# Layer 2's first modulation part summed under layer 1's mix, column chunks on VectorE, and a new order of transfers in a two-layer decoder trunk

## What is computed

```python
cond = jax.nn.silu(c)
for l in range(DEPTH):
    mod = (cond @ w_ada[l] + b_ada[l])[:, None, :]          # w_ada[l]: 1024 x 6144
    sh1, sc1, g1, sh2, sc2, g2 = jnp.split(mod, 6, axis=-1)
    h = x * (1.0 + sc1) + sh1
    u, q_lat, kv_lat, k_rope = jnp.split(h @ w_in[l], split_cols, axis=-1)
    # causal pooling of u, latent attention of q_lat, kv_lat, k_rope, 6 heads
    mixed = jnp.concatenate([pooled, attn], axis=-1) @ w_out[l]
    x = layer_norm(DEEPNORM_ALPHA * x + g1 * mixed, ln1_g[l], ln1_b[l])
    h = x * (1.0 + sc2) + sh2
    ffn = swiglu(h, shared weights) + routed_moe(h, ...)    # 64 experts, top 8
    x = layer_norm(DEEPNORM_ALPHA * x + g2 * ffn, ln2_g[l], ln2_b[l])
```

## Time and profile before

| | |
|---|---|
| median of 3 runs | 1358.78 us (1357.85 to 1361.09) |
| the profiled execution | 1359.6 us |
| its span in the trace | 1357.8 us |
| TensorE busy | 1281.2 us (94%) |
| VectorE busy | 462.8 us (34%) |
| ScalarE busy | 255.1 us (19%) |
| GpSimd busy | 160.9 us (12%) |
| moved by DMA | 495.83 MB, 365 GB/s over the span |

### The profile page before, as it was taken

The page is one execution under the profiler, slowest core; times in us unless marked ns, Lnnn a source line. Parts: engine busy times, 40 slices in busy tenths (PEclk is TensorE's granted clock), DMA queues, the critical chain, the costliest instruction groups (busy, mean ns, idle before and its releaser), DMA issues.

```text
span 1357.8 us, 28824 instructions
## 1 busy us (share of the span) xinstructions
PE 1281.2 (94%) x9667; PEld 796.8 (59%) x9667; DVE 462.8 (34%) x1096; ACT 255.1 (19%) x528; POOL 160.9 (12%) x589
## 2 busy tenths in 40 slices
PE   7989999899799999999898999999999999999995
PEld 3455566566466665666446557666666666656563
DVE  1264542222222222232427355222333222322235
ACT  1213211111111111111123312111111111111113
POOL 0000022111111111112000002012111111111110
PEclk8989999899899999999999999999999999999998
DMA  9998459999999999999989855769989999999992
GB/s 325 351 401 342 191 213 422 419 422 419 422 422 419 421 422 421 371 382 416 387 351 368 356 200 180 332 234 420 421 334 422 421 420 421 421 420 386 394 408 111
DMA packets 86679, 495.83 MB, mean 365 GB/s; under 512 B 14244, under 2 KB 22452, under 8 KB 31816
## 3 DMA queue, kind: packets, MB, share of 16 engines
q1 hardware_dynamic: 86600, 494.66, 90.1%
HBM read 493.55 MB, written 1.08 MB: 364 GB/s over the span
## 4 chain that ended last, share of the span: by engine, by line
PE 85%; DVE 5%; DMA 5%; issue 2%; SPq 1%; ACT 1%; POOL 0%; DVEq 0%; ACTq 0%; POOLq 0%
PE ps L999 31%; PE ps L1021 15%; PE ps L931 9%; PE ps L1042 8%; PE ps L941 4%; PE ps L647 4%; PE ps L864 4%; DMA ring<-in_w_ada 3%; DMA w<-in_w_ada 2%; PE ps L887 2%; DVE acc L1427 1%; PE ps L967 1%; PE ps L1014 1%; PE ps L947 1%; PE ps L830 1%
## 5 line engine op out<-in xcount | busy, mean ns | idle before, releaser
L999 PE MATMUL ps<-ring,w 128*64 128x256 f32 (+1 forms) x3776 | 426.4, 384 | 2.9 <-ACT w L1185 1.8
L999 PEld LDWEIGHTS ps<-ring,w 128*64 128x64 f32 (+1 forms) x3776 | 269.3, 127 | 73.4 <-issue 16.3
L1021 PE MATMUL ps<-ring,w 128*64 128x512 f32 (+1 forms) x944 | 215.0, 597 | 0.0
L999 PE MATMUL ps<-flex,w 128*32 128x256 f32 x736 | 169.2, 389 | 20.0 <-issue 19.7
L999 PE MATMUL ps<-w 128*32 128x256 f32 x736 | 169.7, 390 | 0.0
L1612 DVE SCALAR_TENSOR_TENSOR w<-ps,w 128x256 f32<-128x256 f32 x59 | 28.5, 484 | 384.8 <-PE ps L999 384.8
L931 PE MATMUL ps<-hx,scat 128*128 128x512 f32 x488 | 142.9, 417 | 0.9 <-issue 0.9
L1598 DVE CAST scat<-ps 128x512 fp32r<-128x512 f32 x118 | 81.7, 692 | 164.4 <-PE ps L1021 164.4
L1179 ACT ACTIVATE w<-ps 128x512 f32<-128x512 f32 x122 | 73.0, 598 | 298.8 <-PE ps L931 298.8
L999 PEld LDWEIGHTS ps<-flex,w 128*32 128x32 f32 x736 | 81.0, 112 | 77.5 <-issue 35.3
L1042 PE MATMUL ps<-scat 128*128 128x512 f32 x472 | 123.3, 403 | 0.0
(11 more groups left out here) (259 smaller groups left out, 1252.3 us busy)
## 6 DMA issues: line engine op xcount, KB each, us to landing
ring<-in_w_exp_gate SPq DMA_DIRECT2D x88, 1024.0 KB, 18.3
ring<-in_w_exp_up SPq DMA_DIRECT2D x88, 1024.0 KB, 20.7
ring<-in_w_exp_down SPq DMA_DIRECT2D x88, 1024.0 KB, 20.9
ring<-in_w_ada SPq DMA_DIRECT2D x30, 1024.0 KB, 10.1
flex<-in_w_exp_gate SPq DMA_DIRECT2D x20, 1024.0 KB, 12.4
w<-in_w_exp_gate SPq DMA_DIRECT2D x20, 1024.0 KB, 15.3
flex<-in_w_exp_up SPq DMA_DIRECT2D x20, 1024.0 KB, 14.0
w<-in_w_exp_up SPq DMA_DIRECT2D x20, 1024.0 KB, 17.1
```

Of the source, the lines that this page charges most:

```text
L999: last = mm(ps[unit * g:unit * g + unit, bank, 0:F], hTb[:, kt, unit * g:unit * g + unit], weights(k)[:, kt, :], start=kt == 0, stop=kt == ...
L1021: last = mm(ps[unit * g:unit * g + unit, bank, :], midT[:, f, unit * g:unit * g + unit], down_w(k)[:, f, half * 512:(half + 1) * 512], sta ...
```

## The change

Six things change.

1. In layer 1's start the chunk sums go to VectorE: eight operations of 128x512 per chunk (`scalar_tensor_tensor` into `acc0`), each linked to the one before. `turn_chunk` then adds all 128 partitions up by a product with ones.
2. Layer 2's part 0 is summed on VectorE in layer 1's mix (`next_part`): six of the eight tiles before `norm_stats` of token tile 0, two before that of tile 1. SP issues the tiles in two groups of four (`next_tiles`), one ahead of the stores of the modulation, one behind the column loads. 16 small matmuls behind the last piece of the mix make the columns, in place of the filler matmuls. All of this leaves the step between the layers.
3. The two column loads `g2_col` and `b2_col` move from layer 1's start to just ahead of the second group.
4. VectorE sums the first two tiles of part 1 (`gate_part((0, 1))`) ahead of its pooling and rotary work; `w_out` is loaded in two halves, one behind tile 5 and one behind tile 7 of part 1.
5. TensorE sums tiles 0 and 1 of part 2 between the scores of heads 1 and 2 and of heads 3 and 4, and tile 3 to 7 one in each of the first five heads.
6. The gathered tokens are transposed ahead of the second half of the shared expert's down product; `shmid` lies in `acc0` for that.

The core of the diff:

```diff
@@ SP, end of layer 1's attention and its mix
+                if l == 0:
+                    sp.wait_ge(s["acc0_zeroed"], 2)
+                    sp.dma_start(acc0[0:1, :], b_ada[1:2, 0:ADA_W]).then_inc(s["acc0_bias_in"], 16)
+                    next_tiles((0, 1, 2, 3))
                 store_mod(l, 1)
                 store_mod(l, 2)
                 mod_row(g_row, 2, s["rows1_in"])
...
+                if l == 0:
+                    for dst, src in ((g2_col, lay(ln2_g, 0)), (b2_col, lay(ln2_b, 0))):
+                        sp.dma_start(dst, src.rearrange("a (k p) -> p (a k)", p=P)).then_inc(s["cols2_in"], 16)
+                if l == 0:
+                    next_tiles((4, 5, 6, 7))
                 sp.wait_ge(s["pv_ready"], (l + 1) * H)
@@ SP, weights of a layer
-                ada_tiles(l, 1, (4, 5, 6, 7))
+                ada_tiles(l, 1, (4, 5))
+                load_w_out(0, 4)
+                ada_tiles(l, 1, (6, 7))
+                load_w_out(4, 8)
@@ VectorE, start of layer 1
-                        dve.wait_ge(s["p0_done"], c + 1)
                         part = acc0[:, c * CHUNK_W:(c + 1) * CHUNK_W]
-                        v.tensor_tensor(part, ps[:, 6, :], part, ALU.add).then_inc(s["p0_evicted"], 1)
+                        for kt in range(KT):
+                            if kt % 4 == 0:
+                                dve.wait_ge(p0_landed[2 * c + kt // 4], 32)
+                            ins = v.scalar_tensor_tensor(part, p0_chunk(c)[:, kt].rearrange("p h n -> p (h n)"), c32v[:, kt, 0:1], part,
+                                                         ALU.mult, ALU.add)
@@ VectorE, the mix
+                def next_part(kts):
+
+                    for kt in kts:
+                        n = NEXT_JOB + kt
+                        buf = n % ADA_BUFS
+                        dve.wait_ge(ada_landed[buf], (n // ADA_BUFS + 1) * 16)
+                        ins = v.scalar_tensor_tensor(acc0[:, :], ada_at[buf], c32v[:, kt, 0:1], acc0[:, :], ALU.mult, ALU.add)
+                        ins.then_inc(ada_used[buf], 1)
+                        dve.wait_ge(ada_used[buf], n // ADA_BUFS + 2)
...
                 mod_value(2, slice(0, 64)).then_inc(s["mod_val_ready"], 1)
+                if l == 0:
+                    dve.wait_ge(s["acc0_bias_in"], 48)
+                    next_part(range(6))
                 dve.wait_ge(s["cols_in"], (l + 1) * 64)
...
                 normalise(0, l * 2 * NT + 1).then_inc(s["t_ready"], 1)
+                if l == 0:
+                    next_part((6, 7))
+                    dve.sem_inc(s["p0_done"], 1)
@@ TensorE, behind the mix
-                keep_busy(0, 4)
+                if l == 0:
+                    pe.wait_ge(s["p0_done"], CHUNKS + 1)
+                    for i in range(2 * KT):
+                        last = mm(ps[:, 1, P0_COL + i:P0_COL + i + 1], acc0[:, i * P:(i + 1) * P], ones[:, 0:1], start=True, stop=True)
+                    last.then_inc(s["p0_columns"], 1)
+                else:
+                    keep_busy(0, 4)
@@ TensorE, between the layers
-                    for kt in range(KT):
-                        pe.wait_ge(p0_landed[kt], 48)
-                        for g in range(4):
-                            last = mm(ps[32 * g:32 * g + 32, 6, :], c32v[:, kt, :], next_p0[kt][:, g, :],
-                                      start=kt == 0, stop=kt == KT - 1)
-                    last.then_inc(s["p0_done"], 1)
                     turn_x2(0)
@@ TensorE, shared expert
                     if j == 0:
+                        pe.wait_ge(s["G_ready"], (b0 + l + 1) * 2)
+                        passed(pe)
+                        turn_gathered(b0, 0)
+                        turn_gathered(b0, 1)
                         pe.wait_ge(s["order_read"], l + 1)
```

More of the change, by code:

```diff
@@ L69 @@
 ADA_BUFS = 4
-ADA_JOBS = ((None, 0, 8), (None, 16, 24))
+ADA_JOBS = ((None, 0, 8), (None, 24, 32))
+NEXT_JOB = 16
 CHUNKS = 4
@@ L223, in decoder_trunk @@
         ada = [a.rearrange("p (g n) -> p g n", g=4) for a in ada_at]
-        next_at = [ring[:, i * ADA_W:(i + 1) * ADA_W] for i in range(6)] + [w1[:, 4 * ADA_W:5 * ADA_W], flex[:, 0:ADA_W]]
-        next_p0 = [a.rearrange("p (g n) -> p g n", g=4) for a in next_at]
         def p0_chunk(c):
@@ L538, in _, with load_w_out @@
                     sp.wait_ge(s["x2_ready"], NT)
-                sp.dma_start(wout3, lay(w_out, l).rearrange("a (k p) n -> p (a k) n", p=P)).then_inc(s["wout_in"], 16)
+                def load_w_out(first, end):
+                    src = lay(w_out, l).rearrange("a (k p) n -> p (a k) n", p=P)
+                    sp.dma_start(wout3[:, first:end, :], src[:, first:end, :]).then_inc(s["wout_in"], 16)
                 sp.dma_start(router3, lay(w_router, l).rearrange("a (p k) e -> p (a k) e", k=KT)).then_inc(s["router_in"], 16)
@@ L565, in _ @@
                 sp.dma_start(down_w(3), lay(w_sh_down, l).rearrange("a (k p) d -> p (a k) d", p=P)).then_inc(s["sh_landed"], 16)
+                if l == 0:
+                    for n in range(NEXT_JOB + 4, NEXT_JOB + 7):
+                        sp.wait_ge(ada_used[n % ADA_BUFS], n // ADA_BUFS + 2)
                 for half in range(2):
@@ L823, in _ @@
                 pe.wait_ge(s["jobsA_ready"], (l + 1) * 10)
-                modulation(l, 2, (0, 1))
+                keep_busy(6, 1)
                 pe.wait_ge(s["qrT_ready"], l + 1)
@@ L832, in _ @@
                     last.then_inc(s["scores_done"], 1)
+                    if h in (1, 3):
+                        modulation(l, 2, (h // 2,))
                 def turn_probs(h):
@@ L847, in _ @@
                 modulation(l, 2, (2,))
-                modulation(l, 2, (3,))
                 for h in range(H):
@@ L1448, in _, with norm_stats @@
                     v.tensor_scalar(sP[:, h % 2, P:3 * P], sP[:, h % 2, P:3 * P], rsm[:, h, 1:2], None, ALU.mult).then_inc(s["probs_ready"], 1)
-                def norm_stats(j, done, between=None):
+                def norm_stats(j, done):
                     for half in range(2):
-                        if half and between:
-                            between()
                         q = slice(half * 512, (half + 1) * 512)
```

130 lines of the change are left out of this document (55 added, 75 removed).

## The result

The changed kernel takes **1365.33 us** (median of 9 runs, 1363.51 to 1367.91) against 1357.99 us (9 runs, 1355.08 to 1363.85) for the kernel before, run beside it on the same chip: a ratio of 1.0052 with a 95% interval of 1.0036 to 1.0068, so slower by 0.5%. The profiled execution took 1367.76 us, the third slowest of the nine; its span in the trace is 1365.4.

| us | before | changed | difference |
|---|---|---|---|
| mix of layer 1 starts | 126.73 | 124.73 | -2.0 |
| last transposes of layer 1's mix | 159.29 | 174.99 | +15.7 |
| start of the first gates' matmul (L947, now L944) | 184.55 | 203.30 | +18.8 |
| projection of layer 2 starts | 685.03 | 692.65 | +7.6 |
| mix of layer 2 starts | 775.33 | 785.33 | +10.0 |

What follows compares the result with a forecast made beforehand. TensorE carries 85% of the chain, mostly unchanged expert blocks; layer 1 is bound by bytes up to its mix. +16.5 - 2 x 0.8 - 11.0 = +3.9 us gives 1363 us; range 1349 to 1370, likeliest case 1359 to 1368.

Steps and rivals of the forecast that it cites:

- likeliest case: Whole kernel: the sum as worked, with column loads and clock between their bounds, 1359 to 1368 us; chance 0.57.
- The stall: Layer 1's mix: TensorE waits 20 us for VectorE's norm of tile 0; last transposes at 175.8, 16.5 us later than before.
- Two column loads leave the queue: Layer 1's start: moving them returns 2.16 MB, 5.1 us of the stream; last modulation tile lands at 117.1.
- the order of bytes, not their number: Layer 1 before its mix: moved score sums and halved output weights change only this, so they hide.
- The store behind the tiles: Layer 1's mix: stores wait behind four tiles, SP's two take over 12 us instead of 5; gate row issued at 134.8.
- the second rival: Layer 1's mix: the stores pass the loads, the sixth tile comes at 140, stall 7.7 us, total 1349; chance 0.15.
- The clock: Layer 1's mix, last quarter after the stall: lower TensorE clock adds 2.5 us, bounds 0 and 3.2.
- in place of the filler matmuls: Behind layer 1's mix: sixteen tiny column matmuls lie in the 4.0 us before the last transposes.
- The step between the layers: Between the layers: projection starts 11.1 us sooner without TensorE's sums, fold and column matmuls; 0.8 given back to the clock.
- The earlier turning: Shared expert, both layers: gathered tokens transposed ahead of half its matmuls saves 0.8 us, twice, bounds 0 and 1.8.
- Another 0.7 is won: Layer 2 up to its mix: VectorE's earlier sums win 0.7 us; mix starts 11.0 sooner, at 764.3.
- The projection 4.5 us sooner: Layer 1's start: chunk sums on VectorE end the projection some 4.5 us sooner, but give nothing by itself.

Runs made afterwards that it cites:

- experiment 2: Changed kernel with the two column loads issued behind tiles 4 to 7 instead of in front of them: 1364.7 us, ratio 1.0051 to the kernel before.
- experiment 7: Changed kernel, last part's tiles 0 and 1 summed ahead of scores, tile 3 ahead of weighted sums: 1364.5 us; the wide sums with layer 2's mix weights loaded whole: 1349.4 us.
- experiment 3: Changed kernel with tiles 0 to 3 of layer 2's first part issued behind the stores and columns, together with tiles 4 to 7: 1364.4 us, ratio 1.0049.
- experiment 4: Changed kernel with VectorE summing tiles 4 to 7 between the two halves of the norm of token tile 1: 1356.3 us, ratio 0.998.
- experiment 8: Changed kernel with layer 1's column chunks summed on TensorE again, as in the kernel before: 1366.4 us, ratio 1.0048.
- experiment 1: Changed kernel with layer 2's first part loaded and summed between the layers again and the four wide fillers back in the gap: 1359.7 us, ratio 1.0007.
- the second kernel of 5: Changed kernel with the 32 one-column matmuls moved behind the shared expert's up projection, four wide fillers in the gap: 1367.9 us, ratio 1.0074.
- the wide sums: Changed kernel with experiment 4's order, wide fillers, and four wide matmuls with a block of ones in place of the 32 one-column matmuls: 1354.1 us, ratio 0.9963.
- the last version: The wide sums with layer 2's mix weights issued whole in front of tiles 4 to 7 of the gate part: 1349.4 us, ratio 0.994.

## Why the prediction came out as it did

The sign and the place of the loss were right, and the time lies inside the likeliest case's own range: 1363 forecast, 1365.3 measured, range 1359 to 1368. The difference was not: +3.9 us forecast, +7.6 in the traces and +7.3 by the medians. Two terms of 3.1 us each are missing from it, and smaller ones take 2.5 back. That the stall came out to the us is luck, since a term too low and a term too high cancelled in it. By its steps:

- **The stall.** Foreseen: norm of tile 0 at 161.1, last transposes at 175.8. Measured: 160.6 and 175.0. The inside of it came out otherwise. The last modulation tile landed 4.3 us later than forecast (121.4, not 117.1), and with it came later the mix (124.7, not 120.3, so that TensorE waited 15.1 us, not 20) and the gate row's issue (139.41, not 134.8). The two column loads, which I priced at 5.1 us, cost about 1 (experiment 2). In the sum for the norm the gate row is 4.6 too early and the column loads some 4 too dear. The 1.6 us of trailing engines, which no row gives, are taken off and added again and drop out.
- **The failed step is "Two column loads leave the queue".** I read the 2.16 MB missing from 60 to 70 us as the price of the two loads. With them gone, 60 to 70 us still run at 307 and 282 GB/s (305 and 105 before), so that 1.27 of the 2.16 MB are missing still: most of that hole doesn't go with them. The last tile landed only 0.8 us sooner, not 5.1. A second hole opened at 100 to 105 us (279 GB/s, 1.7 us of the stream), where tile 5's load waits for the buffer of tile 1, whose sum had moved between the scores. I had said that this move changes "the order of bytes, not their number", and had not followed the buffers. And the premise that layer 1 is bound by bytes up to its mix holds only up to the scores. With tiles 0 and 1 summed ahead of them (experiment 7) TensorE still waits 5.74 and 0.58 us for these two, and starts the scores at 99.85; behind that it waits for none of the last three tiles, only 0.36 us each for VectorE's heads, and the mix starts at 126.88. Tiles and heads end together, so making the tiles alone sooner need not give anything.
- **The store behind the tiles** came as foreseen in kind (15.16 us, forecast over 12; the second rival is out, and experiment 3 shows that it is the queue in front).
- **The clock** after the stall: +2.5 forecast, +2.5 measured (0.93 in the transposes, 1.55 in the quarter of the mix), and experiment 4 takes nearly all of it away (1.16 and 7.03 us). In the other traces with the full stall the quarter took 7.62 to 8.91 us, so the exact hit is one execution's; the upper bound of 3.2 should have been 3.0 by its own rows (6.38 - 3.39). What I missed is the second fall, 3.1 us (18.8 at the gates' matmul against 15.7 at the transposes). I had written that the column matmuls lie "in place of the filler matmuls", as if both filled the gap alike. They take the same 3.6 us; only the clock behind them differs. The forecast lacks these 3.1 us.
- **The step between the layers**: -11.1 less 0.8 forecast, -10.9 measured. **The earlier turning**: 0.8 forecast, 1.0 measured, twice.
- **"Another 0.7 is won" in layer 2** was wrong: 2.4 were lost. The halved load of the weights, which I had put down as hidden, took them out of a thin stretch of the stream (experiment 7). That is another 3.1 us that the forecast lacks.
- **The projection 4.5 us sooner**: 1.1 in these two traces, and none that stands out of the spread (experiment 8). VectorE's sums took 0.75 us each, not 0.69, eight with their gaps 6.26 and not 5.8, and the last chunk lands late in any case, so that TensorE waits 4.13 us for them and then runs at the low clock. The conclusion drawn from it, that it is worth nothing, held (experiment 8).

## What to carry to other kernels

When sums are moved under another stage, ask first in which order the engine that does them serves the two: here, in the traces, the same eight sums held the gates' matmul up by 21.0 us with six of them before the norm that TensorE waited for, and by 10.9 with four before it, with no byte moved (182.33 to 203.30 and to 193.20; the medians of the two orders differ by 9.0). When a load is shifted, look for the thin stretch of the stream that it had been filling and for the buffer that its neighbours wait on. And matmuls of one column were no filler here: where the engine's clock matters, let a wide matmul with a block of ones do the sum and pick the columns out of its small result.

## What the runs showed of the hardware

- **Behind 32 one-column matmuls the clock fell from the 2.4 GHz level towards that of 1.2 GHz, with TensorE shown busy up to the fall but for the half us of waiting that the kernel before has too**: to 0.58 in a window of 5 us in the changed kernel, 0.60 with the stall filled, 0.66 in the kernel before with them alone, 0.50 behind wide fillers. It fell, to between 0.50 and 0.74, in all eight traces that have these matmuls in this gap with the clock up before them. With wide matmuls in their place (experiment 1, the second kernel of 5, the wide sums, the last version, and the kernel before) it stayed at 1.00 from 165 to 180 us. The Trainium skill, "TensorE: Matmul & The Clock Gate", section "Part 1: The HAM clock gate (the "warmup" mystery)", says that the gate follows how busy the engine has been; by the busy time of these records (5.00 of 5.00 us in which it was 0.58) the fall can't be foreseen. Why it comes behind these matmuls is not shown here.
- **Behind a short wait the clock differs from execution to execution**: after 3.17 us of idle it was 1.00 from 150 to 155 us (the wide sums), after 3.14 us 0.66 in the last version, where the quarter of the mix then took 8.73 us and not 7.03.
- **A store of 8 KB took 14.66 us behind a backlog of loads**: at the 420 GB/s of that stretch these are 6.2 MB, the four tiles and what was left of the expert weights. With the four tiles behind them the two stores took 9.01 us instead of 15.16.
- **Two column loads of 1024 single elements each landed 3.0 us after their issue** when little was queued, and cost the next tile 1 us. The second held SP for 0.59 us then, for 8.21 behind four tiles (experiment 2), and for 11.40 in the kernel before: the long holds were not its own price.
